# A chunked delta-rule recurrence: the head norm moved to later steps, the matrix to invert built by predicated copies into a buffer with a fixed diagonal

## The reference

```python
def step(S, inp):
    r_t, w_t, k_t, v_t, kk_t, kka_t = inp
    sa = jnp.einsum('bhvk,bhk->bhv', S, kk_t)
    S = (S * w_t[:, :, None, :] - sa[..., None] * kka_t[:, :, None, :] + v_t[..., None] * k_t[:, :, None, :])
    y_t = jnp.einsum('bhvk,bhk->bhv', S, r_t)
    return S, y_t
...
y = head_group_norm(y, lnx_w, lnx_b)      # per token and head: subtract the mean, divide by the deviation, scale, shift
y = (y + bonus) * silu(g)
```

## Time and profile before

| | |
|---|---|
| median of 3 runs | 2113.73 us (2109.63 to 2113.75) |
| the profiled execution | 2113.75 us, of which its span is 2112.0 us |
| busy in the span | PE 2013.4 us (95%), DVE 1418.9 us (67%), ACT 1008.1 us (48%), POOL 174.7 us (8%) |
| PE's granted clock | 0.992 of full speed, mean |
| the recurrence | from 431 us (first products) to about 860 us |
| PE busy in turns 1 to 7 (472 to 812 us) | 292.8 of 340 us |

### The profile page before, as it was taken

The page is one execution under the profiler, slowest core; times in us unless marked ns, Lnnn a source line. Parts: engine busy times, 40 slices in busy tenths (PEclk is TensorE's granted clock), DMA queues, the critical chain, the costliest instruction groups (busy, mean ns, idle before and its releaser), DMA issues.

```text
span 2112.0 us, 42671 instructions
## 1 busy us (share of the span) xinstructions
PE 2013.4 (95%) x16558; PEld 1629.3 (77%) x16558; DVE 1418.9 (67%) x2272; ACT 1008.1 (48%) x1765; POOL 174.7 (8%) x183
## 2 busy tenths in 40 slices
PE   5999999988888889999999999999999999999998
PEld 4877777777777776788888888888667778888886
DVE  7788888876666664555563655799786776445355
ACT  6666666645656665333232332442665434334243
POOL 5230000000233332200000000000000000000000
PEclk9999999999999999999999999999999999999999
DMA  4445555563333322233333333333113322333332
GB/s 121 122 143 164 168 178 183 178 139 74 94 74 75 89 59 82 80 90 99 99 96 98 95 99 90 100 90 100 50 41 100 100 70 81 99 95 95 100 92 78
DMA packets 395952, 215.19 MB, mean 102 GB/s; under 512 B 85136, under 2 KB 374312, under 8 KB 395816
## 3 DMA queue, kind: packets, MB, share of 16 engines
q1 hardware_dynamic: 395608, 213.18, 35.2%
q10 hardware_dynamic: 208, 0.06, 0.0%
HBM read 181.68 MB, written 31.52 MB: 101 GB/s over the span
## 4 chain that ended last, share of the span: by engine, by line
PE 86%; DVE 6%; ACT 3%; issue 3%; DMA 1%; SPq 1%; POOL 0%; DVEq 0%; ACTq 0%; POOLq 0%
PE bank L1911 23%; PE bank L1913 23%; PE bank L1912 23%; PE bank L596 3%; PE bank L573 1%; PE bank L604 1%; PE bank L506 1%; PE bank L547 1%; PE bank L520 1%; PE bank L1108 1%; PE bank L526 1%; ACT inv L821 1%; PE bank L539 1%; DVE inv L922 1%; PE bank L553 1%
## 5 line engine op out<-in xcount | busy, mean ns | idle before, releaser
L1911 PE MATMUL bank<-xl,w_hi 128*128 128x512 f32 x1568 | 615.7, 393 | 3.9 <-DVE xl L2633 2.5
L1912 PE MATMUL bank<-xl,w_lo 128*128 128x512 f32 x1568 | 611.1, 390 | 0.0
L1913 PE MATMUL bank<-xl,w_hi 128*128 128x512 f32 x1568 | 611.0, 390 | 0.0
L1558 ACT ACTIVATE w_hi<-w_raw 128x1024 fp32r<-128x1024 f32 x278 | 293.1, 1054 | 481.9 <-PE bank L1913 477.4
L2202 DVE TENSOR_TENSOR w_lo<-w_raw,w_hi 128x1024 fp32r<-128x1024 f32 x278 | 342.6, 1232 | 48.7 <-ACT w_hi L1558 40.0
L1911 PEld LDWEIGHTS bank<-xl,w_hi 128*128 128x128 f32 x1568 | 294.5, 188 | 76.6 <-issue 9.9
L1913 PEld LDWEIGHTS bank<-xl,w_hi 128*128 128x128 f32 x1568 | 294.8, 188 | 61.9
L1912 PEld LDWEIGHTS bank<-xl,w_lo 128*128 128x128 f32 x1568 | 294.9, 188 | 60.6 <-issue 0.5
L1911 PE MATMUL bank<-xh,w_hi 128*128 128x512 f32 x448 | 183.0, 409 | 10.9 <-DVE xh L2207 10.7
L1913 PE MATMUL bank<-xh,w_hi 128*128 128x512 f32 x448 | 175.5, 392 | 0.0
L1912 PE MATMUL bank<-xh,w_lo 128*128 128x512 f32 x448 | 175.4, 392 | 0.0
(11 more groups left out here) (385 smaller groups left out, 3165.5 us busy)
## 6 DMA issues: line engine op xcount, KB each, us to landing
w_raw<-in_a_w_in SPq DMA_DIRECT2D x64, 512.0 KB, 4.2
w_raw<-in_b_w_in SPq DMA_DIRECT2D x64, 512.0 KB, 4.1
w_raw<-in_w_ffn_up SPq DMA_DIRECT2D x42, 512.0 KB, 4.0
w_raw<-in_w_in SPq DMA_DIRECT2D x36, 512.0 KB, 3.8
w_raw<-in_a_w_out SPq DMA_DIRECT2D x16, 512.0 KB, 4.2
w_raw<-in_b_w_out SPq DMA_DIRECT2D x16, 512.0 KB, 4.0
w_raw<-in_w_ffn_down SPq DMA_DIRECT2D x16, 512.0 KB, 4.1
d_g<-sq SPq DMA_DIRECT2D x16, 256.0 KB, 2.2
```

The source lines that it names most:

```text
L1558: A(w_hi[0:rows, slot, 0:nkb, 0:ncol], w_raw[0:rows, slot, 0:nkb, 0:ncol], ACT.Copy).then_inc(s_hi, units)
L1911: mm(outp, wh, xlo, start=start, stop=False)
L1912: mm(outp, wl, xhi, start=False, stop=False)
L1913: return mm(outp, wh, xhi, start=False, stop=stop)
```

## The change

- The matrix to invert keeps its unit diagonal in the buffer: POOL copies `eyes` into both `nix` buffers once, at the end of the mixing, and DVE then only writes the strictly lower part over it by two predicated copies a group (`set_strict`), with the mask as predicate. So `nix` holds I + L itself, positive, where it held -L; the inverses come out negative, and the factor of `sv` becomes 1 instead of -1.
- The rounding to fp16 moves from DVE to ACT (`rounded`, behind each `turned_out`); DVE makes the first approximation from the fp32 matrix. POOL's low part loses its first instruction.
- In turns 2 to 7 PE's four sums of the head norm stand in steps 9, 10, 13 and 15, and ACT's parts (c: copy, s: square, r: reciprocal deviation; the digit is the tile) in steps 10 to 16. From turn 8 on they stand as before.
- POOL does both low parts of a turn ahead of both finishes.

```diff
--- before.py
+++ after.py
...
@@ -491,6 +493,17 @@
                       13: (0, 5), 14: (1, 4), 15: (0, 6), 16: (0, 7), 17: (1, 5), 18: (1, 6), 19: (1, 7)}
         Y_SPLIT = {1: 0, 3: 1, 5: 2, 7: 3, 9: 4, 10: 5, 11: 6, 13: 7}
         X_BANKS = (2, 3, 5, 6)
+
+        SUMS_LATE = {9: (0, False), 10: (1, False), 13: (0, True), 15: (1, True)}
+        SUMS_EARLY = {1: (0, False), 3: (0, True), 5: (1, False), 7: (1, True)}
+        NORM_LATE = {10: "c0", 11: "c1", 12: "s0", 14: "r0s1", 16: "r1"}
+        NORM_EARLY = {2: "c0s0", 4: "r0", 6: "c1s1", 8: "r1"}
+
+        def sums_of(t):
+            return SUMS_LATE if t < PAIRS else SUMS_EARLY
+
+        def norm_of(t):
+            return NORM_LATE if t < PAIRS else NORM_EARLY
 
         def recurrence_tensor(pe, out_part):
 
@@ -623,6 +636,8 @@
             def newton_v(t, level):
 
                 for n, (a, g) in enumerate(GROUPS):
+                    if level == 1:
+                        pe.wait_ge(R["nix16_made"], 4 * t + n + 1)
                     inverse_ready(t, level - 1, n)
                     diagonal(n, True)
                     each(n, 0, nix16[a], inv2[a][:, 0], start=False).then_inc(R["v_summed"], 1)
@@ -672,12 +687,19 @@
 
             def norm_sum(q, a, squares):
 
+                late = q + 2 < PAIRS
                 if not squares:
                     pe.wait_ge(R["y_bank_read"], 2 * q + 2)
-                    if q or a:
+                    if late and a:
+                        pe.wait_ge(R["centered_copied"], 2 * q + 1)
+                    elif q or a:
                         pe.wait_ge(R["y_rstd_made"], 2 * q + a)
                     mm(bank[4][:], center[:], y0[:, a, :], start=True, stop=True).then_inc(R["centered"], 1)
                 else:
+                    if late and a:
+                        pe.wait_ge(R["y_rstd_made"], 2 * q + 1)
+                    elif late:
+                        pe.wait_ge(R["centered_copied"], 2 * q + 2)
                     pe.wait_ge(R["y_squared"], 2 * q + a + 1)
                     mm(bank[4][:], head_mean[:], ysq[:], start=True, stop=True).then_inc(R["var_summed"], 1)
 
@@ -713,8 +735,8 @@
                             residual(t)
                         elif s == S_LAST:
                             last_inverse(t)
-                    if when(t - 2, PAIRS) and s in (1, 3, 5, 7):
-                        norm_sum(t - 2, s // 4, s % 4 == 3)
+                    if when(t - 2, PAIRS) and s in sums_of(t):
+                        norm_sum(t - 2, *sums_of(t)[s])
 
             q = PAIRS - 1
             out_parts(2, 0, 2)
@@ -752,7 +774,7 @@
                 scaled(rhs[hs, :, :], both(5, 0), 1.0).then_inc(R["rhs_copied"][h], 1)
             elif phase == 1:
                 eng.wait_ge(R["u_summed"], NCH * p + c + 1)
-                scaled(sv[b][hs, :, c, h, :], both(5, 2 * C), -1.0).then_inc(R["u_copied"][h], 1)
+                scaled(sv[b][hs, :, c, h, :], both(5, 2 * C), 1.0).then_inc(R["u_copied"][h], 1)
             elif c < NCH - 1:
                 eng.wait_ge(R["s_summed"], NCH * p + c + 1)
                 decay = st_pc[p % 3][hs, :, c:c + 1]
@@ -832,11 +854,35 @@
                 if g:
                     copy(sv[b][C:P, a, 0, 0, :], v[C:P, 3, 0:C]).then_inc(R["turned_copied"], 1)
 
+            def rounded(t, n):
+
+                a, g = GROUPS[n]
+                cr = slice(4 * g, 4 * g + 4)
+                act.wait_ge(R["nix_made"], 8 * t + 2 * n + 2)
+                copy(nix16[a][:, cr, :], nix[a][:, cr, :]).then_inc(R["nix16_made"], 1)
+
             def y_out(q, half):
 
                 act.wait_ge(R["y_summed"], 2 * q + half + 1)
                 copy(y0[:, :, half * (T // 2):(half + 1) * (T // 2)],
                      bank[7][:].rearrange("p (a t) -> p a t", a=2)).then_inc(R["y_bank_read"], 1)
+
+            def norm_part(q, parts):
+
+                for kind, a in zip(parts[::2], parts[1::2]):
+                    a = int(a)
+                    if kind == "c":
+                        act.wait_ge(R["centered"], 2 * q + a + 1)
+                        if q:
+                            act.wait_ge(R["y_finished"], 2 * q - 1 + a)
+                        copy(yc[a], bank[4][:]).then_inc(R["centered_copied"], 1)
+                    elif kind == "s":
+                        act.wait_ge(R["centered_copied"], 2 * q + a + 1)
+                        A(ysq[:], yc[a], ACT.Square).then_inc(R["y_squared"], 1)
+                    else:
+                        act.wait_ge(R["var_summed"], 2 * q + a + 1)
+                        o(A(yr[a][:], bank[4][:], ACT.Ln, bias=eps[:, 1:2]))
+                        A(yr[a][:], yr[a][:], ACT.Exp, scale=-0.5).then_inc(R["y_rstd_made"], 1)
 
             for t in range(PAIRS + 2):
                 b, q = t % 2, t - 2
@@ -850,6 +896,7 @@
                     if when(t, PAIRS):
                         if s in (1, 3, 5, 7):
                             turned_out(t, s // 2)
+                            rounded(t, s // 2)
                         elif s == 8:
 
                             act.wait_ge(R["turned_copied"], TURNED[3] * (t + 1))
@@ -873,18 +920,7 @@
                                 act.wait_ge(R["t_summed"], 4 * t + n + 1)
                                 copy(tt[b][:, n, 0:4, :], heads(n)).then_inc(R["inverse_made"][0], 1)
                     if when(q, PAIRS):
-                        if s in (2, 6):
-                            a = s // 6
-                            act.wait_ge(R["centered"], 2 * q + a + 1)
-                            if q:
-                                act.wait_ge(R["y_finished"], 2 * q - 1 + a)
-                            o(copy(yc[a], bank[4][:]))
-                            A(ysq[:], yc[a], ACT.Square).then_inc(R["y_squared"], 1)
-                        if s in (4, 8):
-                            a = s // 8
-                            act.wait_ge(R["var_summed"], 2 * q + a + 1)
-                            o(A(yr[a][:], bank[4][:], ACT.Ln, bias=eps[:, 1:2]))
-                            A(yr[a][:], yr[a][:], ACT.Exp, scale=-0.5).then_inc(R["y_rstd_made"], 1)
+                        norm_part(q, norm_of(t).get(s, ""))
                     then(t, s)
 
         def recurrence_vector(dve, o, out_weights):
@@ -902,24 +938,26 @@
                 return a, slice(4 * g, 4 * g + 4), [
                     bank[product_bank(n, h)][:].rearrange("p (c x k) -> p c x k", c=4, x=2) for h in range(2)]
 
-            def negated(t, n):
+            def set_strict(t, n):
 
                 a, cr, (p0, p1) = group(n)
                 dve.wait_ge(R["products_summed"], 4 * t + n + 1)
+                if t == 0 and n == 0:
+                    dve.wait_ge(s_const, 5)
+                if t and n < 2:
+                    dve.wait_ge(R["low_made"], 2 * t - 1 + n)
+                    dve.wait_ge(R["nix16_made"], 4 * t)
                 for hs, p in ((slice(0, C), p0[0:C, :, 0, :]), (slice(C, P), p1[C:P, :, 1, :])):
-                    V.scalar_tensor_tensor(out=nix[a][hs, cr, :], in0=p, scalar=-1.0,
-                                           in1=wide(strict, hs.start, hs.stop, 4), op0=ALU.mult,
-                                           op1=ALU.mult).then_inc(R["nix_made"], 1)
+                    V.copy_predicated(nix[a][hs, cr, :], wide(strict.bitcast(I32), hs.start, hs.stop, 4),
+                                      p).then_inc(R["nix_made"], 1)
 
             def first_steps(t, n):
 
                 a, cr, (p0, p1) = group(n)
-                dve.wait_ge(R["nix_made"], 8 * t + 2 * n + 2)
-                TT(nix16[a][:, cr, :], nix[a][:, cr, :], eyes[:, cr, :], ALU.subtract).then_inc(R["nix16_made"], 1)
                 TT(st_q[t % 2][C:P, a, cr, 0, :], p0[C:P, :, 0, :], wide(strict, C, P, 4), ALU.mult)
                 TT(st_q[t % 2][0:C, a, cr, 2, :], p1[0:C, :, 1, :], wide(strict, 0, C, 4), ALU.mult)
-                dve.wait_ge(R["nix16_made"], 4 * t + n + 1)
-                TT(inv2[a][:, 1, cr, :], nix16[a][:, cr, :], bmask[:, 0, :].unsqueeze(1).to_broadcast([P, 4, C]),
+                dve.wait_ge(R["nix_made"], 8 * t + 2 * n + 2)
+                TT(inv2[a][:, 1, cr, :], nix[a][:, cr, :], bmask[:, 0, :].unsqueeze(1).to_broadcast([P, 4, C]),
                    ALU.mult).then_inc(R["q0_made"], 1)
 
             def masked(t, n):
@@ -966,7 +1004,7 @@
                     if s in (2, 4, 6, 8):
                         masked(t, s // 2 - 1)
                     if s in (0, 2, 4, 6):
-                        negated(t, s // 2)
+                        set_strict(t, s // 2)
                     elif s in (1, 3, 5, 7):
                         first_steps(t, s // 2)
                     elif s == 8:
@@ -1042,16 +1080,14 @@
             def low_part(t, a):
 
                 gp.wait_ge(R["nix16_made"], 4 * t + 3 + a)
-                o(G.tensor_tensor(nix[a][:], nix[a][:], eyes[:], ALU.subtract))
                 G.tensor_tensor(nixlo16[a][:], nix[a][:], nix16[a][:], ALU.subtract).then_inc(R["low_made"], 1)
 
```

(6 more changed lines are left out.)

## The result

The changed kernel took 2122.85 us (median of 6 runs, 2114.84 to 2128.30) beside 2112.70 us of the kernel before on the same chip (6 runs, 2108.09 to 2114.48): a ratio of 1.0049, with a 95% interval of 1.0034 to 1.0065. It is slower, by 10.2 us in the medians. The profiled execution took 2120.44 us with a span of 2118.7, which is 6.7 us more than the profiled execution before.

A forecast was written before the change was run, and what follows sets the result against it. A ring of PE, DVE and ACT was taken to bound the front, PE's short matmuls and code fetch the back. Six late turns +6.4, turn 0 -0.7, turn 1 +0.1: +5.8 on 2113.75, 2119.5 us, range 2111 to 2126.

The forecast's parts named there:

- Front: Steps 0 to 8 of a turn, paced by a PE, DVE, ACT ring: 17.8 instead of 18.57 us, gain 0.77.
- the rounding's delay at the front's end: ACT's rounding, 0.42 us, stands ahead of its last copies, so L520 of step 9 starts about 0.1 us later in turn 1.
- Sums in the back: Four norm sums of 0.95 us on PE at steps 9, 10, 13 and 15: 3.8 us added a turn.
- waits for code: PE's idle time marked "issue" in the back, read as code fetch; three blocks absorb about 0.7 us each, 2.1 a turn.
- the wait for tmp: In the back ACT's copy c1 delays tmp, on which PE's L506 waits: 0.6 us a turn, bounds 0 to 0.6.
- Turn 0: No chain runs beside; without L918 and the collision with GpSimd, DVE's end is shorter: -0.7 us.
- GpSimd and the queues: Finishing, and SP's next st_bv and gates loads, move some 10 us later; the data is used a turn later: free.
- all absorbed: Rival: PE's code stalls in the back take in all 3.8 us of sums and tmp's 0.6: 2107 us, faster; chance 0.22.
- dear copy: Rival: a predicated copy on DVE takes 0.84 us and eats the front's gains: 2127 us, slower; chance 0.14.
- the cancelling: Rival: in the back four blocks absorb and half of tmp's delay falls into a stall: 2113.5 us; chance 0.14.

The follow-up runs named there:

- e4: The changed kernel with ACT's rounding one step later, behind the recurrence copies of steps 2, 4, 6 and 8: 2117.92 us, 1.0029 of the kernel before.
- e10: The kernel before with SP's loads of the next st_bv and gates put behind the next turn's second set of q loads: 2106.23 us, ratio 0.9974.
- e6: The changed kernel with SP's loads of st_bv and gates put behind the next turn's second set of q loads: 2115.95 us, 1.0010 of the kernel before.
- e13: The kernel before with the late norm, matrix as before, and the st_bv and gates loads behind the second set of q loads: 2111.10 us, ratio 1.0002.
- e12: The changed kernel again, unaltered, beside the kernel before on one chip: 2119.77 us, ratio 1.0051.
- e1: The changed kernel with the old matrix part and DVE's rounding put back, so the late norm alone: 2120.46 us, 1.0033 of the kernel before.
- e3: The changed kernel with unread matmuls filling PE's waits in the front of turns 2 to 7: 2120.84 us, 1.0039 of the kernel before.
- e9: The changed kernel with the norm early, the rounding one step later and the st_bv and gates loads behind st_q's: 2109.87 us, 0.9975 of the kernel before.
- e11: The changed kernel with the norm early, the rounding one step later and the loads where the kernel before has them: 2111.97 us, 1.0004 of the kernel before.
- e7: The kernel before with the st_bv and gates loads held until the end of the back in turns 2 to 7: 2118.11 us, ratio 1.0025.
- e8: The changed kernel with the loads behind st_q's and the rounding one step later: 2111.10 us, 0.9986 of the kernel before.

## Why the prediction was right, and where it was not

The forecast was 2119.5 us, slower; the change is slower, and 2122.85 lies in the range of 2111 to 2126. Its cost is 10.2 us, though, where 5.8 were forecast. By its steps:

- **Front.** A late turn was to take 17.8 us to L520 of step 9; four of the six take 17.81 or 17.80, and two 18.40 and 19.73, where the clock is at half for part of them. The predicated copy (444 ns for 0.42 us), the rounding (416 for 0.42) and the first approximation (406 for 0.41) came as taken, and the rounding's delay at the front's end is what e4 gives back.
- **Sums in the back.** The waits for code give back 2.2 us a turn for the 2.1 taken, the wait for tmp is 0.63 for 0.6. With the loads moved in both kernels a late turn grows by 1.5 us under the whole change (e10 to e6, 238.89 to 246.29 us in five turns), up to 0.3 of it clock, and by 1.1 us under the late norm with the old matrix (e10 to e13), for the 1.06 predicted. PE's busy time a turn, which was to stay, grew from 42.71 to 43.84 us with the lower clock.
- **Turn 0** fell from 41.05 to 39.02 us, not by 0.7: before, one more stretch at half clock lay in its front. The granted clock rose from 0.92 to 0.96, worth up to 1.7 of the 2.0 us, so the term itself is not measured.
- **The step that failed** is the one on GpSimd and the queues: the loads of the next st_bv and gates "would issue some 10 us later too", "Free". They issue 12.0 us later in the turn (the finish, which was put at 10 us later, ends 18.1 us later: 25.5 us from the first products before, 43.6 now), and what they fetch is indeed in time. What was not asked is what they would run beside. At the end of the back they come together with PE's waits for code, which become 1.9 to 2.4 us in three turns of five, and in two of these with the clock's fall. Moving them out of there takes 0.4% off the changed kernel (1.0049 and 1.0051 to 1.0010, 0.18 either way).
- **The missing term** is thus the clock: +6.8 us in e12, and +2.7 for the rest, against a sum of +5.8 in which no clock stood. So with the loads late the work cost less than the sum, and the sum left out what is the larger part in e12, e1 and e3 alike; that the time still lies in the range is in part luck. Five turns of the profile say the same: 1.75 us more a turn, up to 1.36 of it clock. With the loads moved in both kernels (e10 to e6) the sum does better: the whole change costs 0.36% (0.12 either way), +5.4 us of it rest and +1.8 clock's share. Why the rest is lower with the loads late was not traced, and the spread of the runs leaves room for chance.

Of the rivals, **all absorbed** falls: 10.8 us of waits for code are left beside the sums, and the turns grew. The Trainium skill, Runtime: NRT & Kernel Launch, section on instruction fetch mechanics, has the crossing from block to block mostly hidden. The kernel before does not agree: by the 254 instructions a block that the prediction counts, turns 2 to 6 have some 45 crossings, and 27 of them show a wait, and in e10, the fastest, 25 do. With the sums in the back it comes nearer to it: 11 of the changed kernel's crossings show one. The **dear copy** falls with its 444 ns, the cancelling with both ratios.

**What stays open.** The late norm and the place of the loads don't add up in one way only. The loads' move gains 0.26% in the kernel before, 0.31% under the late norm alone and 0.4% under the whole change; the differences between these are within what the intervals leave open. In the clock's share they are larger, -1.2, -5.0 and -6.2 us, but the spread of the runs hardly settles that either. How a load delays code (in the transfers, or in memory) was argued from the places alone, and no run tries it by itself. What brings the clock down is not settled either: it follows long waits for code at 618.29 and 669.50, but not at 536.38 and 693.39, the longest wait (before 568.48) has no fall behind it, and e3's fill did not bring the time back.

## What to carry to other kernels

When a wait is moved, follow what is queued behind it to the place where it will run, and ask what that place can't bear; "its data is in time" answers only half. In a stretch in which an engine runs through code nearly as fast as it arrives, a megabyte of loads (four of 256 KB a turn) was dear here, and a better place for it was where the engine waits for something else: moving four transfers a turn gained 0.26% of the kernel before (e10, 2106.23 us, by its ratio the fastest kernel measured here together with e9); no other single edit of this study gained more. A shorter front is not yet a shorter turn: e11's fronts are 0.84 us shorter, and the back took it. And compare granted clocks of all runs ahead of explaining a difference of some tenths of a per cent.

## What the runs showed of the hardware that was not expected

PE's waits for code change with the place of the data transfers. In turns 2 to 6 they come to 22.0 us in the kernel before, to 24.5 with its loads late (e7) and to 16.4 with them in the front (e10); under the late norm to 10.8, 11.8 and 11.2 with the loads late (the changed kernel, e12, e1) and to 6.8 and 6.3 with them in the front (e6, e13). With the later rounding the loads' move takes them from 15.1 to 7.7 (e4, e8) and from 21.4 to 18.1 (e11, e9). These are sums of one profile each. The longest single wait follows the place less simply: 2.1 to 2.9 us under the late norm with the loads late (the changed kernel, e12, e1, e4), 1.2 or less with them in the front in e6, e8, e10 and e13, but 2.4 us in e9 (before 737.63), whose loads stand in the front, too. And a masked write is hardly dearer here than a product: 444 ns for 64x256 out of PSUM, beside 427 ns for the masked product of the same columns (L957).
